# Expert choice by maxima and ranks, places in fp32r, fewer filler products, another bank and an earlier table load in the tail

## What is computed

```python
pg = softmax(xt @ rg_w + rg_b); g_sel = argmax(pg); pg_top = max(pg)      # 4 groups
le = einsum('nd,gde->nge', xt, re_w) + re_b                               # 8 experts in each
le_sel = einsum('nge,ng->ne', le, one_hot(g_sel))
pe = softmax(le_sel); top_v, top_i = top_k(pe, 2); top_v /= sum(top_v)
comb = pg_top * one_hot(g_sel) x sum_k(one_hot(top_i) * top_v)
for gi in range(4):
    h = silu(xt @ e_wg[gi]) * (xt @ e_wu[gi])                             # 8 experts, FF 512
    out += (h * comb[:, gi]) @ e_wd[gi]
y = rmsnorm(h + out, final_g)
```

## Time and profile before

| | |
|---|---|
| runs (us) | 1259.4, 1260.37, 1264.03; median 1260.37 |
| the profiled execution | 1261.07, span 1259.2 |
| granted TensorE clock, mean | 0.989 |
| TensorE / VectorE / ScalarE / GpSimd busy | 97% / 47% / 29% / 5% |
| HBM read | 268.7 MB |
| chain that ended last | PE 88%, DVE 8%, ACT 1%, DMA 1% |

### The profile page before, as it was taken

How to read it: one execution, slowest core, us unless ns; L and a number is a source line. 1 busy time by engine, 2 the same in 40 slices (tenths; PEclk the granted TensorE clock), 3 DMA queues, 4 the chain that set the end, 5 groups by cost and what they waited for, 6 DMA issues and landing times.

```text
span 1259.2 us, 22942 instructions
## 1 busy us (share of the span) xinstructions
PE 1226.1 (97%) x10014; PEld 889.2 (71%) x10014; DVE 594.5 (47%) x974; ACT 360.5 (29%) x624; POOL 59.9 (5%) x99
## 2 busy tenths in 40 slices
PE   8999899999999999999999999999999999999995
PEld 8889888988898789999999886444444434444442
DVE  5346865554364543333333233454554545454544
ACT  5445343444324542222223321111111111111114
POOL 3100000001000100000000001000000000000000
PEclk9989999999999999999999999999999999999997
DMA  8210102302324823322324676999999999999992
GB/s 246 68 34 1 36 5 70 104 3 73 107 66 125 262 79 92 85 76 78 98 85 169 265 310 262 414 418 420 419 419 420 419 419 419 419 419 418 420 380 76
DMA packets 110206, 273.78 MB, mean 217 GB/s; under 512 B 22309, under 2 KB 69623, under 8 KB 85530
## 3 DMA queue, kind: packets, MB, share of 16 engines
q1 hardware_dynamic: 106234, 265.21, 55.6%
q0 software_dynamic: 2560, 4.73, 1.0%
q10 hardware_dynamic: 1312, 2.36, 0.5%
HBM read 268.72 MB, written 7.22 MB: 219 GB/s over the span
## 4 chain that ended last, share of the span: by engine, by line
PE 88%; DVE 8%; ACT 1%; issue 1%; DMA 1%; SPq 0%; DVEq 0%; ACTq 0%
PE bank L658 16%; PE bank L665 9%; PE bank L1507 7%; PE bank L803 6%; PE bank L1440 6%; PE bank L1442 6%; PE bank L1441 6%; PE bank L1567 2%; PE bank L1569 2%; PE bank L1568 2%; DVE yl L1090 2%; PE bank L850 2%; PE bank L1726 1%; PE bank L797 1%; PE bank L1680 1%
## 5 line engine op out<-in xcount | busy, mean ns | idle before, releaser
L658 PE MATMUL bank<-slot,xs 128*64 128x512 f32 x512 | 233.0, 598 | 0.9 <-DVE xs L1034 0.9
L659 PE MATMUL bank<-slot,xs 128*64 128x512 f32 x512 | 233.0, 598 | 0.0
L658 PEld LDWEIGHTS bank<-slot,xs 128*64 128x64 f32 x512 | 65.0, 136 | 124.8 <-issue 121.6
L1440 PE MATMUL bank<-xnh,wh 128*128 128x256 f32 (+1 forms) x448 | 133.1, 297 | 0.6 <-DVE mt L3071 0.6
L1441 PE MATMUL bank<-xnl,wh 128*128 128x256 f32 (+1 forms) x448 | 132.6, 296 | 0.0
L1442 PE MATMUL bank<-xnh,low 128*128 128x256 f32 (+1 forms) x448 | 132.6, 296 | 0.0
L1064 DVE TENSOR_TENSOR h<-h,bank 128x1024 f32<-128x1024 f32 (+1 forms) x73 | 86.4, 1214 | 89.0 <-PE bank L803 89.0
L2623 DVE TENSOR_TENSOR low<-ring,wh 128x1536 fp32r<-128x1536 f32 (+1 forms) x45 | 89.9, 2004 | 78.2 <-ACT wh L2262 70.9
L665 PE MATMUL bank<-slot,ht 128*64 128x512 f32 x512 | 118.6, 606 | 2.0 <-DVE yl L1090 2.0
L900 ACT ACTIVATE sg<-bank,csr 64x512 f32<-64x512 f32 x32 | 21.9, 685 | 270.5 <-PE bank L659 270.5
L1440 PEld LDWEIGHTS bank<-xnh,wh 128*128 128x128 f32 x448 | 85.0, 190 | 1.3 <-issue 1.2
(11 more groups left out here) (539 smaller groups left out, 2347.0 us busy)
## 6 DMA issues: line engine op xcount, KB each, us to landing
slot<-in_e_wg_dram SPq DMA_DIRECT2D x64, 1024.0 KB, 21.1
slot<-in_e_wu_dram SPq DMA_DIRECT2D x64, 1024.0 KB, 23.2
slot<-in_e_wd_dram SPq DMA_DIRECT2D x64, 1024.0 KB, 23.3
ring<-in_w_in_dram SPq DMA_DIRECT2D x13, 1024.0 KB, 5.4
ring<-in_w_in_dram SPq DMA_DIRECT2D x24, 512.0 KB, 4.2
ring<-in_w_branch_dram SPq DMA_DIRECT2D x24, 256.0 KB, 4.6
kvs<-in_cache_mem_k_dram SPq DMA_DIRECT2D x8, 512.0 KB, 5.7
kvs<-in_cache_mem_v_dram SPq DMA_DIRECT2D x8, 512.0 KB, 5.7
```

The costliest lines, as they stand in the source:

```text
L658: pe.matmul(out[64:128, :], tok, wg[:, FF * k:FF * k + FF], start=(k == 0), stop=(k == KD - 1))
L659: mm = pe.matmul(out[0:64, :], tok, wu[:, FF * k:FF * k + FF], start=(k == 0), stop=(k == KD - 1))
L1440: pe.matmul(part, w_h, xh_(k, cols), start=(k == 0), stop=False)
```

## The change

- The choice: for the groups and each of the two experts, a reduction to the maximum, a subtraction, a mark (difference equals zero, times a falling rank `rev4` or `rev8`), and a reduction of the marks to the highest rank, all five tiles at a time. One-hots come from the rank, and those over 32 experts from the product of the group's and the expert's. Expert numbers (`eid`) are computed from the ranks behind `place1`. The copy to `lg8` goes. `rev4` and `rev8` are made ahead of the choice, from `iota_f`.
- `sel`, `before_r` and `ones_r` are fp32r, so the six products of the places are fp32r.
- The 16 filler products behind the lists go; the 30 and the 6 stay.
- In `out_act` the copy of the last turned tile stands ahead of the last square.
- SP issues expert 2's down weights (the ninth slot) only when the gathers of experts 0 and 1 have landed.
- `down(31)` writes bank 2 (`HT_BANK`) instead of 3 and doesn't wait for `yl` of expert 30.
- The Sqrt of a constant moves from behind the last SiLU to behind the branch of the general path.

```diff
-        XG_BANK, HT_BANK, Y_BANK = 1, 2, 3
+        XG_BANK, HT_BANK = 1, 2
+
+        def y_bank(e):
+            return HT_BANK if e == EX - 1 else 3
...
-            for n in range(3):
+            for n in range(2):
                 load(2, n)
+            for n in range(2):
+                sp.wait_ge(gathered[n], 16)
+            load(2, 2)
...
+            turned(4)
             square(4)
-            turned(4)
...
-                dve.memset(lg8[:, :, :], -1e30)
-                dve_t.done(dve.memset(sel[:, :, :], 0.0), "clear")
+                dve.tensor_copy(before_r[:, :], before[:, :])
+                dve.tensor_copy(ones_r[:, :], ones[:, :])
+                dve_t.done(dve.memset(sel[:, :, :].bitcast(F32), 0.0), "clear")
...
-                dve.tensor_copy(iota_f[:, :], iota_i[:, :])
+                dve_t.done(dve.tensor_copy(iota_f[:, :], iota_i[:, :]), "iota")
+                dve_t.wait(dve, "iota")
+                dve.tensor_scalar(rev4[:, :], iota_f[:, 0:NG], -1.0, float(NG), ALU.mult, ALU.add)
+                dve.tensor_scalar(rev8[:, :], iota_f[:, 0:NE], -1.0, float(NE), ALU.mult, ALU.add)
...
-            pe.matmul(places, before[:, :], sel[:, :, :], start=True, stop=False, skip_group_check=True)
+            pe.matmul(places, before_r[:, :], sel[:, :, :], start=True, stop=False, skip_group_check=True)
...
-            idle_products(pe, 7, 16)
             dve_t.wait(pe, "lists")
...
-                if e >= 1:
+                if 1 <= e < EX - 1:
                     dve_e.wait(pe, ("yl", e - 1))
...
-                if e == EX - 1:
-                    act_e.wait(act, ("silu", e))
-                    act.activation(rstd[:, 5:6], ones[:, 0:1], ACT.Sqrt)
...
             general_act(act)
+            act.activation(rstd[:, 5:6], ones[:, 0:1], ACT.Sqrt)
             dve_f.wait(act, "clear")
...
-            def top(src, n):
-
-                for t in range(5):
-                    last = dve.max(mx[n][:, t, :], src[:, t, :])
-                seq(last)
-                for t in range(5):
-                    last = dve.max_index(mi[n][:, t, :], mx[n][:, t, :], src[:, t, :])
-                seq(last)
-                seq(dve.tensor_copy(ix[:, n, :], mi[n][:, :, 0]))
+            def best(n, src, size, rev):
+                seq(dve.tensor_reduce(top[:, n, :], src, AX.X, ALU.max))
+                seq(dve.tensor_tensor(gap[:, :, 0:size], src, wide(top[:, n, :], size), ALU.subtract))
+                seq(dve.scalar_tensor_tensor(mark[:, :, 0:size], gap[:, :, 0:size], 0.0, rev[:, :].unsqueeze(1).to_broadcast([128, 5, size]),
+                                             ALU.is_equal, ALU.mult))
+                seq(dve.tensor_reduce(rank[:, n, :], mark[:, :, 0:size], AX.X, ALU.max))
...
+            def pick(k):
+                return dve.tensor_tensor(ohe[:, k, :, :], rev8[:, :].unsqueeze(1).to_broadcast([128, 5, NE]), wide(rank[:, 1 + k, :], NE), ALU.is_equal)
+
+            def spread(k):
+                return dve.tensor_tensor(oh12[:, k, :, :].rearrange("p t (g e) -> p t g e", e=NE),
+                                         ohg[:, :, :].unsqueeze(3).to_broadcast([128, 5, NG, NE]),
+                                         ohe[:, k, :, :].unsqueeze(2).to_broadcast([128, 5, NG, NE]), ALU.mult)
+
+            dve_t.wait(dve, "dg")
+            best(1, les[:, :, :], NE, rev8)
+            seq(pick(0))
+            seq(dve.scalar_tensor_tensor(le2[:, :, :], ohe[:, 0, :, :], -1e30, les[:, :, :], ALU.mult, ALU.add))
+            spread(0)
+            best(2, le2[:, :, :], NE, rev8)
+            seq(pick(1))
+            seq(spread(1))
...
-            for k in range(2):
-                last = dve.tensor_scalar(odd_i[:, k, :], mi[1 + k][:, :, 0], 1, None, ALU.bitwise_and)
-            seq(last)
+            seq(dve.tensor_copy(rank_i[:, :, :], rank[:, 1:3, :]))
+            seq(dve.tensor_scalar(odd_i[:, :, :], rank_i[:, :, :], 1, None, ALU.bitwise_and))
```

More of the change, by code:

```diff
@@ L359, in route_tile @@
             return t
-        lg8 = route_tile("lg8", [128, 5, 8])
         les4 = route_tile("les4", [128, 5, NG, NE])
@@ L364, in build @@
         le2 = route_tile("le2", [128, 5, 8])
-        ltmp = route_tile("ltmp", [128, 5, 8])
-        mx = [route_tile(f"mx{n}", [128, 5, 8]) for n in range(3)]
-        mi = [route_tile(f"mi{n}", [128, 5, 8], U32) for n in range(3)]
-        ix = route_tile("ix", [128, 3, 5])
+        top = route_tile("top", [128, 3, 5])
+        gap = route_tile("gap", [128, 5, 8])
+        mark = route_tile("mark", [128, 5, 8])
+        rank = route_tile("rank", [128, 3, 5])
+        rank_i = route_tile("rank_i", [128, 2, 5], U32)
+        ohe = route_tile("ohe", [128, 2, 5, NE])
+        rev4 = route_tile("rev4", [128, NG])
+        rev8 = route_tile("rev8", [128, NE])
         ohg = route_tile("ohg", [128, 5, NG])
@@ L396, in build @@
         vsel = sb("vsel", [128, 2, NT], F32, late_at)
+        before_r, ones_r = (sb(n, [128, 128], F32R, late_at + at) for n, at in (("before_r", 1536), ("ones_r", 2048)))
         yg = sb("yg", [128, 512], F32, z3 + 55296)
@@ L599, in build @@
         act_t = Steps(sem("act_t"), ["root", "exp_g", "exp_e", "codes"])
-        dve_t = Steps(sem("dve_t"), ["clear", "sumsq", "ms", "rstd", "lg", "dg", "sel", "places", "rows", "code", "lists", "addr", "de", "c12", "cw", "scales"])
+        dve_t = Steps(sem("dve_t"), ["clear", "sumsq", "ms", "iota", "rstd", "dg", "sel", "places", "rows", "code", "lists", "addr", "de", "c12", "cw", "scales"])
         dve_l = Steps(sem("dve_l"), ["zeros", "saved", "normed", "even", "gather0", "scatter0", "gather", "scatter"] + [("more", t, k) for t in range(5) for k in range(2)] + ["restored"])
@@ L841, in down @@
                     pe.wait_ge(eslot_loaded[(3 * e + 2) % NSLOT][f], 16 * ((3 * e + 2) // NSLOT + 1))
-                    mm = expert_out(pe, psum[Y_BANK], ht[e % 2], slots[(3 * e + 2) % NSLOT], range(2 * f, 2 * f + 2), e % 2)
+                    mm = expert_out(pe, psum[y_bank(e)], ht[e % 2], slots[(3 * e + 2) % NSLOT], range(2 * f, 2 * f + 2), e % 2)
                 pe_m.done(mm, ("d", e))
@@ L965, in moe_dve @@
             seq(dve.tensor_reduce(les[:, :, :], les4[:, :, :, :].rearrange("p t g e -> p t e g"), AX.X, ALU.add))
-            top(les, 1)
-            seq(dve.tensor_tensor(ltmp[:, :, :], iota5(NE), wide(ix[:, 1, :], NE), ALU.is_equal))
-            seq(dve.scalar_tensor_tensor(le2[:, :, :], ltmp[:, :, :], -1e30, les[:, :, :], ALU.mult, ALU.add))
-            top(le2, 2)
-            for k in range(2):
-                last = dve.scalar_tensor_tensor(eid[:, k, :], ix[:, 0, :], float(NE), ix[:, 1 + k, :], ALU.mult, ALU.add)
-            seq(last)
-            for k in range(2):
-                last = dve.tensor_tensor(oh12[:, k, :, :], iota5(EX), wide(eid[:, k, :], EX), ALU.is_equal)
-            seq(last)
+            def pick(k):
[12 more added lines that the diff above has]
+            seq(spread(1))
             dve.tensor_tensor(sel[:, 0:4, :], oh12[:, 0, 0:4, :], oh12[:, 1, 0:4, :], ALU.add)
@@ L998, in moe_dve @@
                                          ALU.is_equal), "rows")
+            for k in range(2):
+                last = dve.scalar_tensor_tensor(eid[:, k, :], rank[:, 0, :], -float(NE), rank[:, 1 + k, :], ALU.mult, ALU.subtract)
+            seq(last)
+            seq(dve.tensor_scalar(eid[:, :, :], eid[:, :, :], float(NE * (NG + 1)), None, ALU.add))
             dve_t.done(dve.scalar_tensor_tensor(code12[:, :, :], row12[:, :, :], float(EX), eid[:, :, :], ALU.mult, ALU.add), "code")
```

20 lines of the change are left out of this document (9 added, 11 removed).

## The result

| | before | changed |
|---|---|---|
| median (us), executions | 1259.4, 7 | 1249.97, 7 |
| lowest to highest | 1257.26 to 1264.03 | 1248.74 to 1255.97 |
| the profiled execution | 1261.07, span 1259.2 | 1249.23, span 1247.5 |
| granted TensorE clock, mean | 0.989 | 0.993 |

The ratio changed to before is 0.9932, with a 95% interval from 0.9916 to 0.9948: 8.6 us less (6.5 to 10.6). The forecast was 1249.5 us, and faster by more than 0.5%.

What follows compares the result with a forecast made beforehand. TensorE was taken to bound the expert stage, its weights arriving in time. The first part's 4.7 us and the tail's 6.2 made 10.9 off 1261.07: predicted 1249.5 us, range 1246.8 to 1253.8.

Steps and rivals of the forecast that it cites:

- Entry: Start of the choice: the last square goes behind the copy, so the first addition comes at 748.1, 0.6 us lost.
- The choice: First addition to the places' first product: 5.56 us removed, 3.6 added, net 1.95 saved, leaving 6.86 us.
- The places: Six products behind the choice: next VectorE step 1.15 us behind the first, range to 1.6, instead of 2.5.
- first product: First gate-and-up product of expert 0: near 766.9 instead of 772.7; 5.8 us earlier, 4.1 after one clock fall of 1.7.
- rival 1: Choice and experts: weight stream becomes the bound or clock falls twice; first part gives 2.5 us or less; chance 0.15.
- The limit of the stream: Expert stage: its end can move by 4.5 us of stream plus 0.8 of slack, 5.3 at most.
- The gathers and the ninth slot: Loads ahead of expert 0: gathers take 3.2 us with a free queue; ninth slot lands 7.7 later, stream moves 4.5.
- Rival 4: Weight loads: a slow second gather holds SP and delays the whole stream, making the kernel slower; chance 0.04.
- The tail: Behind the last experts: bank 3.1, table load 2.55 and tile 4's products 0.55 us, together 6.2 saved.
- 2: Tail: first Square still loads a table after the branch, or tile 4 stays behind; 2.6 to 3.2 us lost; chance 0.08.
- 3: The first part, up to the experts, gives nothing and only the tail's gain remains: 1254.2 us; chance 0.09.
- 5: Tail: a drain goes with each ScalarE table load, so the tail gives 2.7 us more: 1246.8; chance 0.04.

Runs made afterwards that it cites:

- more filler: Changed kernel with 9 instead of 6 filler products behind the places and 2 behind the lists: 1248.18 us, ratio 0.9902 to before.
- again: The changed kernel measured once more with no edit, ten executions: 1251.03 us, ratio 0.9938 to before.
- best: The more filler kernel with the last square ahead of the last copy, as before the change: 1247.87 us, ratio 0.9912 to before.
- The tail alone: Kernel before with only the bank and wait of the last down product and the Sqrt as changed: 1254.42 us, ratio 0.9957.
- no_tail: All but the tail: the changed kernel with both tail edits (bank with its wait, Sqrt) undone: 1255.99 us, ratio 0.9956 to before.
- preload_undo_f: The more filler kernel with the Sqrt of a constant back behind the last SiLU, ahead of the branch: 1252.07 us, ratio 0.994 to before.

## Why the prediction was right, and where it was wrong

**Entry: right.** 0.6 us lost was forecast. The addition moved from 4.82 to 5.33, 0.5, and undoing it gave 0.5 back.

**The choice: right.** Forecast 6.86 us from first addition to the places; measured 12.08 - 5.33 = 6.75, and 2.04 saved in the direct comparison, where I had 1.95. Counting instructions by the durations of their neighbours was good to 0.1 us in a chain of some twenty.

**The places: right, the upper bound a little low.** Next VectorE step 1.15 behind the first product, measured 1.04. The bound of full fp32 passes was 1.55; measured 1.71.

**Codes behind the lists: right; first product: right for this profile.** 5.8 less one fall of 1.7 was to be 4.1; it was 4.38. That the clock would fall with the gaps ahead of and behind the lists (forecast 1.4 and 0.7, measured 1.08 and 0.65) was right too, and more filler shows it from the other side.

**How many falls: one in the profiles, open for the mean.** I took the price of one, 1.7, and for the whole part 4.7, the middle between one fall and the limit. Both profiles of the changed kernel have one. More filler, with none, gains 24.06 to 29.97 in the choice, 5.9, and 6.0 in the tail (6.3 in most others): 12, and its ratio gives 12.3. The ratios of the changed kernel give 8.6 and, again, 7.8, which is 3.7 to 4.5 less and would be two falls and more. But each ratio's interval reaches 2.0 to 2.5 us to each side, and other kernels say less. `best` has the filler and gains 11.1, 10.6 without its 0.5 for the order, which is 2.0 to 2.8 above the changed kernel: between one fall and two. The tail alone gives 5.4 and all but the tail 5.5, together 10.9, which is nearer to one fall (from the profiles 4.5 + 6.4) than to two (3.3 + 6.4). So rival 1's "the clock falls twice" is seen in one profile and neither shown nor excluded for the mean. The Trainium skill (TensorE: Matmul & The Clock Gate, Part 1: The HAM clock gate) says of the products at a kernel's start that the number of them at half clock differs from run to run of one kernel; far from the start the executions here differ too, with codes of 4.05 and 4.52 us in two profiles of this kernel. I had quoted that page for whether the clock falls. What it says there is of an idle TensorE in general; that it falls with gaps of 1.08 and 0.65 us is shown by these rows alone.

**The limit of the stream: wrong, in both its terms.** The prediction had "the weight stream moves by 4.5", "From there on it is bound by bandwidth", and "Slack 0.8 us", so 5.3 at most. More filler moved the end of the stage by 6.0 and nothing waited. The first term held for the changed kernel, where the first half of expert 31's up weights landed 4.5 us earlier behind the start of the choice; it was no bound, since with more filler it landed 6.1 earlier, with the ninth slot issued no sooner. The changed kernel's stream still had holes (348 GB/s), and its reloads follow the experts. The slack was misread: at 1218.84 TensorE begins step 3 of expert 31 and not the half that landed at 1218.0, which is first used at 1220.61. The first half is the tight one, landed at 1185.18 + 27.8 = 1212.98 for a product at 1214.77: 1.8 us instead of 0.8, and 1.7 in the changed kernel. For the changed kernel the limit did not matter. But it was one end of 4.1 to 5.3, and the middle of that happened to lie near the profile's 4.5: that is luck.

**The gathers and the ninth slot: right.** The first gather took 3.2, the ninth slot 6.1 (I had 7.7 for two loads and took the first reload for 4.5 earlier; it was issued 4.4 earlier, 29.28 against 33.66). What I left out is what the move is worth with early lists: 2.25 us of wait, and the falls behind it. Rival 4, a slow gather that holds SP, found no support: with the free queue these took 3.0 to 3.3.

**The tail: right, 6.33 for 6.2, but one term is of the execution.** Up to the last addition the bank is worth 3.16 (I had 3.1) and the preload 2.53 (2.55), and the cover of 0.9 ahead of the first square was 0.90. The rest is tile 4: 19.57 - 18.83 = 0.74 between before and `no_tail`, up to the last addition. I had put it at 0.55 for products that come earlier and no longer run at half clock; in `no_tail`, with these products left where they were and the clock up, it was gone as well (13.13 + 3.16 + 2.53 is all of the 18.83). So it is a fall of the clock in the profiled execution of before, which other executions of before need not have.

**Rivals.** 2 fell (one table load left), 3 fell (the first part gave 4.5), 5 fell.

**The number.** The two profiles are 11.7 us of span apart, of which 0.85 lie ahead of the change. The sum of 10.9 against the execution of 1261.07 was 0.9914, just outside the measured interval from 0.9916: the forecast time fitted better than the forecast gain, because the executions of before in this comparison lay 1 us under those of the prediction (1259.4 against 1260.37). That too is luck.

## What to carry to other kernels

Taking filler out and adding just enough of it are not the same: put the products back that fill each gap up to its releaser and no further; here five of them were worth 1.5 us in the profile and 2 to 4.5 by the ratios, whose intervals are as wide as that; the falls that they prevent differ from execution to execution, and one profile shows one of these. When you read how much slack a load has, find the first product that uses it, and look at every load: here the second half's product was misread and the first half had less. When a chain gets shorter, look which transfer now has to be early and give it a free queue, as here the gather before the ninth slot. Load a table in the same stretch of code, behind the branch, in which its function is used.

## What the hardware showed beyond the expected

- Two idle stretches of 1.08 and 0.65 us, with forty tiny products of 1.72 between, came with a fall to 1.2 GHz in all four profiles of kernels that have them, at some time between the last of these products and 1.6 us into the codes, and it cost 1.71, 1.71, 3.42 and (with a wait for a gather in it) 6.81 us. With 0.42 or less and none there was no such fall in six profiles of six that have no longer gap.
- The same gap does not always do the same: behind 2.24 us before's tile 4 ran at 1.2 GHz, behind 2.23 us it ran at 2.4 GHz in `no_tail` and in `preload_undo_f`.
- One wait of 2.17 us for a gather cost 5.0 us in all, with the half clock behind it over products that run at full clock otherwise.
- A gather took 3.0 to 3.3 us with a free queue and 4.8 to 7.4 beside bulk loads.
- 4.3 us of delay at the start of a stream that then moved 419 GB/s for over 400 us came out as 1.7 us of stage: 0.6 made up in earlier holes, 1.9 of slack at the tightest load.
